# A two-stage network of 512 tokens on one core: the loads of the beginning, four places of the first stage and the end in another order

## What is computed

```
block 1, layers i = 0, 1:
    a = rms_norm(h, pre_mix_norm[i])
    m = hgrn2_mixer(a) if i == 0 else mla_mixer(a)    # 8 recurrent heads / 16 latent-attention heads
    h = h + rms_norm(m, post_mix_norm[i])
    h = h + rms_norm(relu(rms_norm(h) @ w1)**2 @ w2, post_mlp_norm[i])
    h = h + rms_norm(sigmoid(h @ w_ple_gate[i]) * (p[i] @ w_ple_proj[i]), ple_norm[i])
block 2:
    h = h + hybrid_mixer(rmsnorm(h)); h = h + cross_attention(rmsnorm(h), rmsnorm(mem))
    h = h + conv_ffn(rmsnorm(h));     return rmsnorm(h, norm_final_g)
mla_mixer: cq, ckv, k_rope = split(a @ w_in, [384, 640]); cq, ckv normalised; 16 heads of
    softmax((q_nope @ k_nope.T + rope(q_rope) @ rope(k_rope).T) * 192**-0.5) @ v, then @ w_o
```

## Time and profile before

| | us |
|---|---|
| three runs | 2370.27, 2370.6, 2368.69 |
| median | 2370.27 |
| the profiled execution, its own time | 2372.49 |
| its span in the trace | 2370.6 |
| mean granted clock of TensorE over the span | 0.989 |

### The profile page before, as it was taken

The page is one execution under the profiler, slowest core; times in us unless marked ns, Lnnn a source line. Parts: engine busy times, 40 slices in busy tenths (PEclk is TensorE's granted clock), DMA queues, the critical chain, the costliest instruction groups (busy, mean ns, idle before and its releaser), DMA issues.

```text
span 2370.6 us, 27451 instructions
## 1 busy us (share of the span) xinstructions
PE 2291.2 (97%) x10372; PEld 1857.8 (78%) x10372; DVE 1271.2 (54%) x1820; ACT 648.5 (27%) x1190; POOL 1568.0 (66%) x1530
## 2 busy tenths in 40 slices
PE   7999989999999899999999999999999999999998
PEld 6888877888887677777778888878767787888886
DVE  6674727145245666256372454458875444626354
ACT  3343433101013345245231010132345232202112
POOL 7556556877776545544668777769425947878784
PEclk9999999999999899999999999999999999999999
DMA  5222222333332211211324333323212322333332
GB/s 162 76 71 80 72 79 73 112 97 97 98 98 76 59 35 36 71 42 32 97 73 128 98 99 111 98 76 116 71 37 80 111 67 89 96 97 97 98 96 73
DMA packets 110868, 200.13 MB, mean 84 GB/s; under 512 B 12305, under 2 KB 18705, under 8 KB 110737
## 3 DMA queue, kind: packets, MB, share of 16 engines
q1 hardware_dynamic: 107568, 194.72, 27.4%
q10 hardware_dynamic: 3168, 3.67, 0.5%
HBM read 196.24 MB, written 2.10 MB: 84 GB/s over the span
## 4 chain that ended last, share of the span: by engine, by line
PE 87%; DVE 6%; POOL 4%; ACT 2%; issue 1%; DMA 0%; SPq 0%; DVEq 0%; POOLq 0%
PE bank L469 26%; PE bank L471 25%; PE bank L470 25%; POOL wL L2612 2%; POOL wH L2610 1%; DVE bank L1834 1%; DVE h L1826 1%; PE bank L998 1%; PE bank L502 1%; PE bank L864 1%; DVE tmp L1826 1%; PE bank L869 1%; PE bank L870 1%; PE bank L865 1%; PE bank L866 1%
## 5 line engine op out<-in xcount | busy, mean ns | idle before, releaser
L2612 POOL TENSOR_TENSOR wL<-raw,wH 128x512 fp32r<-128x512 f32 (+2 forms) x731 | 1000.7, 1369 | 60.9
L2610 POOL TENSOR_SCALAR wH<-raw 128x512 fp32r<-128x512 f32 (+2 forms) x731 | 531.2, 727 | 616.4 <-PE bank L471 523.6
L469 PE MATMUL bank<-aH,wH 128*128 128x512 f32 x1376 | 547.0, 398 | 19.2 <-DVE aL L1834 9.6
L471 PE MATMUL bank<-aH,wL 128*128 128x512 f32 x1376 | 537.5, 391 | 0.0
L470 PE MATMUL bank<-aL,wH 128*128 128x512 f32 x1376 | 537.4, 391 | 0.0
L469 PE MATMUL bank<-uH,wH 128*128 128x512 f32 x960 | 375.7, 391 | 5.6 <-DVE uL L1826 5.6
L470 PE MATMUL bank<-uL,wH 128*128 128x512 f32 x960 | 374.5, 390 | 0.0
L471 PE MATMUL bank<-uH,wL 128*128 128x512 f32 x960 | 374.5, 390 | 0.0
L469 PEld LDWEIGHTS bank<-aH,wH 128*128 128x128 f32 x1376 | 258.9, 188 | 78.7 <-issue 13.1
L470 PEld LDWEIGHTS bank<-aL,wH 128*128 128x128 f32 x1376 | 259.0, 188 | 57.0 <-issue 4.1
L471 PEld LDWEIGHTS bank<-aH,wL 128*128 128x128 f32 x1376 | 258.9, 188 | 54.7
(11 more groups left out here) (315 smaller groups left out, 3202.3 us busy)
## 6 DMA issues: line engine op xcount, KB each, us to landing
raw<-in_ws SPq DMA_DIRECT2D x699, 256.0 KB, 2.6
raw<-in_ws SPq DMA_DIRECT2D x24, 192.0 KB, 2.3
h<-in_xT SPq DMA_DIRECT2D x4, 512.0 KB, 7.3
E<-in_memT ACTq DMA_DIRECT2D x16, 128.0 KB, 2.6
out<-c_F SPq DMA_DIRECT2D x8, 256.0 KB, 2.1
tmp<-in_pT ACTq DMA_DIRECT2D x4, 256.0 KB, 3.2
raw<-in_ws SPq DMA_DIRECT2D x8, 128.0 KB, 2.1
g_hc<-in_cst SPq DMA_DIRECT2D x1, 640.0 KB, 9.2
```

The source lines that it names most:

```text
L469: P.e.matmul(o, lH, rH, start=start, stop=False, skip_group_check=skip)
L471: return P.e.matmul(o, lL, rH, start=False, stop=stop, skip_group_check=skip)
L2610: G.e.tensor_scalar(H, x, 1.0, 0.0, MUL, ADD).then_inc(*G.did("wH", n))
L2612: G.e.tensor_tensor(L, x, H.bitcast(F32), SUB).then_inc(*G.did("w", n))
```

## The change

In seven places the order of the work changes; the arithmetic stays.
1. The beginning: 16 columns of gains come first, then weight piece 0, x in eight DMAs of one tile with piece 1 behind the fourth, then pieces 2, 3 and 4 between constants, vectors, gate bounds and masks. ScalarE makes eight high parts and then eight squares, VectorE eight low parts and then six sums. TensorE does two output tiles before the norm's sum. GpSimd no longer waits for the vectors.
2. The recurrence's end: steps 0 | `recur(7)` | 1, 2 | `outputs(7)` | 3 | norm's sum | 4 to 7; ScalarE's table load stands ahead of `recur(7)`.
3. The ple gate's end: the square of tile 7 goes to VectorE; in layer 1 half of the 96 matmuls stands ahead of the norm's sum.
4. The attention's beginning: the squares of cq get tiles of their own in `m_P[0]` and come earlier; the values of heads 0 to 3 stand ahead of the rotary key, key 0 behind the rotation, and the second rotary pair is loaded there; head 0's scores begin with all parts without rotation.
5. Rotary pairs are loaded and turned in odd heads, their high and low parts made in the even head that follows (`rotated`), with `m_qr` twice.
6. Head 7: head 8's query and key, the pair of heads 10 and 11 and its rotation come before the values of head 7, the scores of head 8 before the output projection; GpSimd divides head 6 before and head 7 after the two pieces of head 8. Keys 8 and 9 come in pieces of their own.
7. The end: tiles 5, 6 and 7 of the last down-projection run by halves of the tokens, and the norm's sum, root, products and output DMAs follow per half; ScalarE multiplies the gains in, and tiles 0 to 3 and 4 to 6 are one product and one DMA each per half.

The diff, cut to its core (the new order of ScalarE's program in the attention mirrors that of TensorE's):

```diff
-    keys(0)
     rope(0)
     query(0)
+    keys(0)
+    rope(2)
     for hd in range(16):
         if hd % 8 != 7:
             head(hd + 1)
         if hd % 8 not in (0, 7):
...
-        if hd % 2 == 0 and hd < 14:
-            rope(hd + 2)
+        if hd % 2 and hd < 12:
+            rope(hd + 3)
         if hd % 8 == 7:
-            divided[len(out) + 1] = hd - 1
-            divided[len(out) + 5] = hd
-            mla_out(hd // 8)
+            divided[len(out) + (hd == 15)] = hd - 1
             if hd == 7:
                 head(8)
+            divided[len(out) + (5 if hd == 15 else 2)] = hd
+            mla_out(hd // 8)
...
                     project(head + 1, 2)
                 else:
                     lin = three_open([("hg_w_out", 0, 128 * o) for o in range(3)], [("ho", o) for o in range(3)])
-                    for k in range(5):
-                        three_step(lin, k, uH, uL, y1_ready)
+                    out_steps(0)
                 recur(head)
                 if head < 7:
                     project(head + 1, 0)
                 else:
-                    three_step(lin, 5, uH, uL, y1_ready)
-                    three_step(lin, 6, uH, uL, y1_ready)
+                    out_steps(1, 2)
                 outputs(head)
                 if head < 7:
                     project(head + 1, 3)
+                else:
+                    out_steps(3)
                 stat_end("hs", head, tiles=1, tail=False, freed=(V, "on", head))
                 if head == 3:
                     project_v(1)
-            three_step(lin, 7, uH, uL, y1_ready)
+            out_steps(4, 5, 6, 7)
             three_give(lin, *[(A, "F", "ho", o) for o in range(3)])
             P.also("end hgrn")
...
+                    memory_keys(0)
                 stat_end("ple", i, adds=f"n{i}")
                 P.also("end ple", i)
                 if i == 1:
-                    for o in (0, 2):
-                        memory_keys(o)
+                    memory_keys(2)
                 P.wait_ge(A, "end ple", i)
                 P.wait_ge(V, "end ple", i)
...
-            stat_end("cq", tiles=3, tail=False, freed=(V, "cn", 2))
+            b = take("stat", "cq")
+            P.wait_ge(V, "sum", ("cq",))
+            P.e.matmul(b.ap[:, :], ones, m_P[0][:, 0, :], start=True, stop=True).then_inc(*P.did("stat", "cq"))
+            give(b, V, "cn", 2)
...
             P.also("kr1")
             give(b1, V, "kr1")
             give(b2, V, "kr2")
-            values_in(0)
-            key_in(0)
             rope_in(0)
             query_in(0)
             rotate(0)
+            key_in(0)
+            rope_in(2)
             scores(0)
             for hd in range(16):
-                ahead, turn = hd % 8 != 7, hd % 2 == 0 and hd < 14
+                ahead, turn = hd % 8 != 7, hd % 2 == 1 and hd < 12
                 if ahead:
                     heads_in(hd + 1)
                 if turn:
-                    rope_in(hd + 2)
+                    rope_in(hd + 3)
                 turned(hd)
                 if ahead:
                     scores(hd + 1)
+                elif hd == 7:
+                    heads_in(8)
                 if turn:
-                    rotate(hd + 2)
+                    rotate(hd + 3)
+                elif hd == 0:
+                    rotate(2)
                 values(hd)
                 if hd == 7:
+                    scores(8)
                     mla_out(0)
-                    heads_in(8)
-                    scores(8)
                 if hd % 4 == 3 and hd < 15:
                     values_in(hd // 4 + 1)
...
-                downs("w_down_2", 0, ks, True, lambda o: ("cd", g, o), lambda o: (V, "h cd", g, o), cu_ready)
...
+            last = [block("w_down_2", 0, ks, ((128 * o, 128),)) for o in (5, 6, 7)]
+            for half in range(2):
+                c = half_cols(half)
+                for o in (5, 6, 7):
+                    b = take("cd", 2, o, half)
...
+                        i = three(b.ap[:, 0:256], H, L, uH[:, k, c], uL[:, k, c], k == 0, k == 5)
...
+                    if half and o == 5:
+                        final_sum(0)
+            final_sum(1)
...
             exp_table()
-            A.wait_ge(vs_in)
+            A.wait_ge(gains_in)
             for k in range(8):
-                A.wait_ge(x_in[k // 2])
+                A.wait_ge(x_in[k])
                 do(aH[:, k, :], h[:, k, :], ACT.Copy, scale=vv("pre_mix_norm", k)).then_inc(*A.did("a1H", k))
-                square(("a1",), k, h[:, k, :])
+            for k in range(8):
+                if k > 2:
+                    A.wait_ge(V, "sum", ("a1",), k - 2)
+                do((sums if k == 0 else (tmp[0], sq)[k % 2])[:, :], h[:, k, :], ACT.Square).then_inc(*A.did("sq", ("a1",), k))
+            squares_end[0] = ("a1",)
...
                 sigmoid_g(head)
                 if head < 7:
                     sigmoid_f(head + 1, 1)
+                else:
+                    exp_table()
                 recur(head)
...
-                    square(("ple", i), o, F[:, o, :])
+                    if o < 7:
+                        A.wait_ge(V, "Fg", i, o)
+                        square(("ple", i), o, F[:, o, :])
+                exp_table()
+                squares_end[1] = (P, "stat", "ple", i)
...
+            query_square(0)
+            query_square(1)
+            rstd(256, "ckv")
+            query_square(2)
+            latent(3)
+            latent(4)
...
-            def rotate(hd):
+            def rotated(hd):
                 A.wait_ge(V, "qr", hd)
-                if hd:
-                    A.wait_ge(P, "ms", hd - 1, 3)
+                if hd > 2:
+                    A.wait_ge(P, "ms", hd - 3, 3)
                 for i in range(2):
-                    j = do(m_qr[i][half_rows(i), :], tmp[1][half_rows(i), :], ACT.Copy)
+                    j = do(m_qr[hd // 2 % 2][i][half_rows(i), :], tmp[1][half_rows(i), :], ACT.Copy)
...
-            for o in range(8):
+            def gain(o, c):
+                do(c_F[:, o, c], h[:, o, c], ACT.Copy, scale=vv("norm_final_g_2", o)).then_inc(*A.did("gain", o, c.start))
...
+            for half in range(2):
+                c = half_cols(half)
+                for o in (5, 6, 7):
+                    A.wait_ge(V, "h cd", 2, o, half)
+                    A.wait_ge(V, "sum", *((("final",), 4) if o == 5 else (("final", half), o - 1)))
+                    do(sq[:, c], h[:, o, c], ACT.Square).then_inc(*A.did("sq", ("final", half), o))
+                    if o < 7:
+                        gain(o, c)
...
                     if 0 < o < 7:
                         add_squares(("ple", i), o)
+                V.wait_ge(V, "Fg", i, 7)
+                V.wait_ge(V, "sum", ("ple", i), 6)
+                tt(sq[:, :], F[:, 7, :], F[:, 7, :], MUL).then_inc(*V.did("sq", ("ple", i), 7))
...
+            add_query_squares(1)
+            normed(3)
+            add_query_squares(2)
+            normed(4)
+            normed_low(3)
+            normed_low(4)
             V.wait_ge(P, "kr")
             tt(F[0:64, 5, :], bk("kr")[0:64, :], r[0:64, :], MUL).then_inc(*V.did("kr"))
-            for k in range(3):
-                normed(k, turned_key(k))
-            V.wait_ge(V, "kr3")
-            V.wait_ge(A, "krH")
-            low(m_krL[:, :], F[:, 6, :], m_krH[:, :]).then_inc(*V.did("krL"))
+            normed(0)
+            normed(1)
+            normed_low(0)
+            normed(2)
+            normed_low(1)
+            normed_low(2)
+            turned_key()
...
+            def rotated(hd):
                 V.wait_ge(V, "qr", hd)
                 V.wait_ge(A, "qrH", hd)
                 for i in range(2):
-                    j = low(m_qr[i][half_rows(1 - i), :], tmp[1][half_rows(i), :], m_qr[i][half_rows(i), :])
+                    x = m_qr[hd // 2 % 2][i]
+                    j = low(x[half_rows(1 - i), :], tmp[1][half_rows(i), :], x[half_rows(i), :])
...
+                    rotate(hd + 3)
+                elif hd == 0:
+                    rotate(2)
+                elif hd % 2 == 0 and hd < 14:
+                    rotated(hd + 2)
                 values(hd)
+                if hd == 0:
+                    rotated(2)
                 if hd == 7:
-                    heads_in(8)
                     scores(8)
...
+            def add_half(o, half):
+                c = half_cols(half)
+                V.wait_ge(P, "cd", 2, o, half)
+                tt(h[:, o, c], h[:, o, c], bk("cd", 2, o, half)[:, 0:256], ADD).then_inc(*V.did("h cd", 2, o, half))
+            def sum_half(o, half):
+                c = half_cols(half)
+                V.wait_ge(A, "sq", ("final", half), o)
+                V.wait_ge(V, "sum", *((("final",), 4) if o == 5 else (("final", half), 5)))
+                tt(sums[:, c], sums[:, c], sq[:, c], ADD).then_inc(*V.did("sum", ("final", half), o))
...
+                if part == 2:
```

(52 more changed lines are left out.)

206 lines of the change are left out of this document (128 added, 78 removed).

## The result

The changed kernel took 2333.74 us (median of four runs, 2332.70 to 2335.03) beside 2370.43 of the kernel before; the ratio is 0.9845, 95% interval 0.9828 to 0.9862. The forecast was 2337, range 2326 to 2350. The profiled execution took 2332.70, its span is 2330.9; that is 39.7 us less than the span of the earlier trace rows, where the medians are 36.7 apart, since one of the two profiled executions was among the slower and the other the fastest of its kernel.

A forecast was written before the change was run, and what follows sets the result against it. TensorE bounds the kernel, busy 2291.2 of 2370.6 us. Terms 6 + 2 + 0 - 1.5 + 13 + 5 + 7 + 2 = 33.5 us off 2372.5 gave 2339; the median, 2.2 lower, 2337; range 2326 to 2350.

The forecast's parts named there:

- the rivals: Four: new waits 2348 us, 0.18; everything covered 2330, 0.07; small loads slow 2342, 0.04; key chain binds every head 2379, 0.03.
- the rival's: Loads of the beginning: 256 KB tiles at half of 408 GB/s, third piece at 16.9 us, kernel 2342 us; chance 0.04.
- no head waits for its key: Denies the rival that the key chain binds in every head: 14 heads lose 42 us, kernel 2379 us; chance 0.03.
- The beginning: Loads and first two output tiles up to the norm's sum: 6 us won, bounds 3 and 8.
- The recurrence's end: Output projection steps placed anew around the last head's recurrence: 2 us won, bounds -3 and 5.
- priced at 3.1 us: Recurrence's end: loss taken for the stretch at half clock behind the new 4.3 us wait.
- The ple norm: Square of tile 7 moved to VectorE: layer 0 0 us, bounds -0.5 and 0.5; layer 1 -1.5, bounds -4 and 1.
- the term of -1.5: Ple norm of layer 1: 48 matmuls put the norm's chain 3.5 us later, 1.5 us lost, bounds -4 and 1.
- The attention's beginning: Query norm, rotation and clock up to the first transposes: 13 us won, bounds 9 and 15.
- 1.2 us of new wait: Attention's beginning: first transposes keep 3.4 us of cover against an estimated 4.6 us chain, so 1.2 us lost.
- Rotary pairs and head 7 to 8: Waits for m_knL: 5 us won, bounds 3 and 5; waits for aL and head 8's key: 7, bounds 5 and 7.3.
- The end: Last three tiles by halves of the tokens: 2 us won, bounds 0 and 3.5; TensorE ends 0.9 us later.

The follow-up runs named there:

- end_whole: The changed kernel with the end as before: whole tiles 5 to 7, eight products with the gain and eight DMAs of 256 KB; 2334.86 us.
- piece_late: The changed kernel with weight piece 1 loaded behind the eighth tile of x instead of the fourth; 2334.96 us.
- sum_first: The changed kernel with TensorE's second output tile behind the norm's sum again, loads and order of ScalarE and VectorE as changed; 2341.67 us.
- values_late: The changed kernel with the values of heads 0 to 3 on TensorE behind the two matmuls that turn the rotary key; 2333.02 us.
- rec_gate_late: The changed kernel with head 7's gate sigmoid and both table loads (ScalarE) and its product (VectorE) behind the recurrence's copies; 2328.77 us.

## Why the prediction was right, and where its steps were off

**Right by mechanism.** The seven parts lie where the forecast had them, and each named wait went. The forecast's sum was 33.5 us, the two spans differ by 39.7 and the medians by 36.7. None of the rivals came about: 256 KB tiles moved at much the same rate (297 GB/s from 2.5 to 9.0 us and 387 from 9 to 15, against 279 and 408 with 512 KB pairs before), and the third piece reached GpSimd at 12.97 where 12.4 was forecast and 16.9 was the rival's. The Trainium skill's rule of at least 1 MiB per DMA ("DMA: Bandwidth & Descriptors", Rules for kernel authors) is not borne out by these rates. And no head waits for its key.

**The beginning**: 6 forecast, 6.2 in this trace (5.7 by the middle of the ten). Its steps held: piece 1 was there at 9.16 (9.2 forecast), the second tile ended at 21.4 (21.6), the tile behind the sum began at 24.19 (24.1). Errors cancel in it: the six adds took 8.2 us with their waits for ScalarE's squares instead of 7.0, the low parts ended 0.8 earlier, and the sum on TensorE took 1.4 instead of 1.7. That loads and cover each win nothing alone, in the changed order of ScalarE and VectorE, was implied by the working and not said.

**The recurrence's end**: 2 forecast, 4.1 measured. The new wait was 4.0 for the 4.3 forecast. The clock behind it was priced at 3.1 us. In the changed kernel's trace it cost 1.7 (3.4 us at 0.50); in the nine further traces with this wait the stretch was 3.4 us in four and 6.8 in five, and with 6.8 the part won 2.7 to 3.3 us. So the price is no error that one trace can show, and the 4.1 is partly luck. That the wait can be brought down to 0.6 by moving the gate's sigmoid was not seen.

**The ple norm**: VectorE's square took 1.63 us, not the 1.16 of an add's mean: layer 0 lost 0.6, just outside its bound. In layer 1 the term of -1.5 was too low: 0.5 was won. The step that failed is that TensorE would idle up to 6 us in one piece, with a longer stretch at 0.50. It waited 3.3 us for GpSimd in two pieces (TensorE's timeline, changed kernel), with the same stretch of 3.4 us as before, where it had waited 1.8 for the square and 2.1 for GpSimd; the order by itself costs 0.4.
```profile
1573.01 0.50 PE L581 MATMUL bank<-aH,wH 128*128 128x512 f32 x1 [1.64 <-POOL wL L2777]
...
1575.39 0.79 PE L581 MATMUL bank<-aH,wH 128*128 128x512 f32 x1 [1.65 <-POOL wL L2777]
```

**The attention's beginning**: 13 forecast, 15.2 measured. The step that failed is "1.2 us of new wait" ahead of the first transposes; they waited 0.2 (TensorE's timeline, changed kernel):
```profile
828.82 1.64 PE L916 MATMUL bank<-cs,m_P 128*128 128x128 f32 x13 [0.20 <-POOL m_P L2784]
```
Another 0.6 us was a wait for m_qnL at 836.31 that the forecast did not count. That the values stand ahead of the rotary key covers nothing; the nope parts ahead of the rotary ones do cover, with 0.9 us to spare.

**Rotary pairs and head 7 to 8**: 6.2 and 7.8 where 5 and 7 were forecast, both above their bounds (5 and 7.3). The term that was mis-sized is the price of a wait. Six waits for m_knL went between these heads, 5.1 us as listed, but each delays TensorE by more than its listed length, which leaves out the modelled end of the matmul before it. Here 0.91 is listed, and the start comes 1.07 later than four transposes 0.11 apart would let it (TensorE's timeline, kernel before):
```profile
867.75 0.60 PE L878 MATMUL bank<-cs,m_P 128*128 128x128 f32 x4
869.25 0.47 PE L864 MATMUL bank<-m_knH,m_qnH 128*128 128x512 f32 x1 [0.91 <-DVE m_knL L1826]
```
The six delays make 6.1. In head 7 the same excess is 0.3, and the stretch at 0.50 is 3.4 us long, which may be worth 1.7 and not 1.5. No run undid the order of head 7, or the query's squares alone; these two are read from the traces of before and after only. So for most of the 15.2 and the 7.8, the two largest parts, it is shown that the named waits and stretches are gone, and not by an experiment which of the moves did it.

**The end**: 1.9 for 2; undone, it gives 1.6. TensorE lost 1.7 instead of 0.9, since its 256-column matmuls start every 0.12 us there (window of the changed kernel, the first half's sum among them) and not every 0.114:
```profile
2308.00:2322.00 14.00, 14.00 (x115) 13.86 (x114) 6.10 (x12) 5.74 (x13) 1.71 (x3) 1.00 0.08 27
```
The chain behind it won 3.3: 1.3 in the norm and 2.9 in the products, less 1.0 that the output DMAs take longer (from the last product to the end of the span 3.7 us instead of 2.7 in end_whole). The forecast had 1.4, 2.5 and 0.8.

## What to carry to other kernels

In this kernel an early load won only when the engine that asks for it had nothing else to wait for, and a cover won only when its own data were there: cost the two together, as one chain. When work is moved away from in front of a stage, read the program order of every engine that feeds the stage: here a sigmoid and two table loads of ScalarE stood in front of a 0.5 us copy, and putting them behind it won 4.9 us at its place, more than three of the seven parts of the change. Price a new wait as itself plus the stretch at half clock behind it: behind one and the same wait of 2.0 us it cost nothing, 1.7 or some 3 us.

## What was not expected of the hardware

The granted clock fell where the work and the waits had not changed. Both kernels pass the same 57 us of the mixer of block 2 (from 1702.47 and 1663.04) with starts that keep their distance within 0.03 us, the same waits of 0.38 and 1.99 included; then the next eight matmuls take 3.65 us before and 5.34 after:
```profile
1759.35 0.39 PE L980 MATMUL bank<-d_kH,d_qH 64*128 64x256 f32 x2 [1.99 <-DVE uL L1826]
...
1760.17 3.65 PE L998 MATMUL bank<-F 128*128 128x512 f32 x8
```
```profile
1719.89 0.39 PE L1022 MATMUL bank<-d_kH,d_qH 64*128 64x256 f32 x2 [1.99 <-DVE uL L1928]
...
1720.72 5.34 PE L1040 MATMUL bank<-F 128*128 128x512 f32 x8
```
In the fourteen traces of this case the stretch behind this wait was absent in five (before, end_whole, piece_late, sum_first, values_late), 3.4 us in four and 6.8 in five. Behind the ple norm of layer 0, with the same wait of 3.8 us, it was 6.8 or 10.2. Each kernel has one trace, so the traces alone do not part chance from a shift in time. The times of single executions speak for chance: the four of rec_gate_late took 2326.01 and 2327.31 us at a mean granted clock of 0.997, and 2330.24 and 2330.96 at 0.994. So one trace tells that a wait may cost clock, not how much, and a difference of 1.7 or 3 us at such a place cannot be put down to an edit by it.
